# Plain FFN phases of a transformer on one core: up products with the tokens as weights, their result turned later

## The reference, cut to what matters

```python
D_MODEL, SEQ, D_FF = 1024, 256, 2816

def swiglu(h, wg, wu, wd):
    return (jax.nn.silu(h @ wg) * (h @ wu)) @ wd

h = modulate(rms_norm(x, ln_ffn1[i]), sh1, sc1)
x = x + 0.5 * g1[:, None, :] * swiglu(h, ffn1_wg[i], ffn1_wu[i], ffn1_wd[i])
```

## Time and profile before

| what | us |
|---|---|
| median of 3 runs | 1723.72 (1723.26 to 1723.75) |
| the profiled execution, its own time | 1719.21 |
| its span, first to last instruction | 1717.5 |
| TensorE busy in the span | 1690.1 (98%) |
| VectorE busy | 1395.2 (81%) |
| ScalarE busy | 908.7 (53%) |
| mean DMA traffic over the span | 257 GB/s |

### The profile page before, as it was taken

The page is one execution under the profiler, slowest core; times in us unless marked ns, Lnnn a source line. Parts: engine busy times, 40 slices in busy tenths (PEclk is TensorE's granted clock), DMA queues, the critical chain, the costliest instruction groups (busy, mean ns, idle before and its releaser), DMA issues. The chain is left out here.

```text
span 1717.5 us, 35012 instructions
## 1 busy us (share of the span) xinstructions
PE 1690.1 (98%) x13871; PEld 1649.3 (96%) x13871; DVE 1395.2 (81%) x1785; ACT 908.7 (53%) x1274; POOL 327.8 (19%) x517
## 2 busy tenths in 40 slices
PE   7999999999999999999999999989999999999999
PEld 6999999999999999999999999989999998799998
DVE  6777898788779977898987798779988997787655
ACT  3433367764345634366633457657444567774443
POOL 6111110011112111120111125530111132300000
PEclk9999999999999999999999999999999999999999
DMA  9999967649998899977799965235999882358550
GB/s 338 369 378 331 328 206 265 204 157 351 337 338 286 287 328 316 337 251 260 276 337 341 334 229 196 100 123 171 338 339 329 255 215 69 110 173 288 178 171 24
DMA packets 266302, 440.78 MB, mean 257 GB/s; under 512 B 19278, under 2 KB 201758, under 8 KB 266072
## 3 DMA queue, kind: packets, MB, share of 16 engines
q1 hardware_dynamic: 224968, 290.67, 51.1%
q0 software_dynamic: 41200, 148.71, 23.5%
q10 hardware_dynamic: 32, 0.01, 0.0%
HBM read 423.59 MB, written 17.31 MB: 257 GB/s over the span
## 5 line engine op out<-in xcount | busy, mean ns | idle before, releaser
L2949 DVE TENSOR_TENSOR lo<-raw,hi 128x2048 fp32r<-128x2048 f32 (+2 forms) x251 | 565.6, 2255 | 169.4 <-ACT hi L2774 168.5
L2774 ACT CAST hi<-raw 128x2048 fp32r<-128x2048 f32 (+2 forms) x266 | 497.8, 1874 | 373.0 <-PE dacc L2441 181.6
L2439 PE MATMUL up<-operand_hi,hi 128*128 128x256 f32 x1952 | 552.8, 283 | 1.4 <-DVE lo L2949 1.4
L2440 PE MATMUL up<-operand_lo,hi 128*128 128x256 f32 x1952 | 552.3, 283 | 0.0
L2441 PE MATMUL up<-operand_hi,lo 128*128 128x256 f32 x1952 | 552.3, 283 | 0.0
L2439 PEld LDWEIGHTS up<-operand_hi,hi 128*128 128x128 f32 x1952 | 374.4, 192 | 2.2 <-DVE lo L2949 2.0
L2441 PEld LDWEIGHTS up<-operand_hi,lo 128*128 128x128 f32 x1952 | 374.5, 192 | 0.0
L2440 PEld LDWEIGHTS up<-operand_lo,hi 128*128 128x128 f32 x1952 | 374.5, 192 | 0.0
L2439 PE MATMUL dacc<-act_hi,hi 128*128 128x256 f32 x976 | 276.8, 284 | 0.2 <-DVE act_lo L3183 0.2
L2441 PE MATMUL dacc<-act_hi,lo 128*128 128x256 f32 x976 | 275.9, 283 | 0.0
L2440 PE MATMUL dacc<-act_lo,hi 128*128 128x256 f32 x960 | 270.5, 282 | 0.0
(11 more groups left out here) (496 smaller groups left out, 2907.5 us busy)
## 6 DMA issues: line engine op xcount, KB each, us to landing
ada<-in_ada_w_dram POOLq DMA_DIRECT2D x224, 512.0 KB, 6.2
raw<-in_ffn_wg_dram SPq DMA_DIRECT2D x88, 512.0 KB, 6.0
raw<-in_ffn_wu_dram SPq DMA_DIRECT2D x88, 512.0 KB, 5.6
raw<-in_ffn_wd_dram SPq DMA_DIRECT2D x88, 512.0 KB, 5.3
raw<-in_ffn_w_up_dram SPq DMA_DIRECT2D x88, 512.0 KB, 4.7
raw<-in_ffn_w_down_dram SPq DMA_DIRECT2D x46, 512.0 KB, 4.6
raw<-in_hg_w_in_dram SPq DMA_DIRECT2D x32, 512.0 KB, 4.8
fold_scratch<-ada_acc POOLq DMA_DIRECT2D x28, 512.0 KB, 6.9
```

Source lines behind the costliest of these rows:

```text
L2439: pe.matmul(o, stat[0], mov[0], start=start, stop=False, skip_group_check=True)
L2440: pe.matmul(o, stat[0], mov[1], start=False, stop=False, skip_group_check=True)
L2774: last = act.copy(put(slab(hi, s, SPL)), take(slab(raw, s, RAW)))
L2949: last = dve.tensor_tensor(put(slab(lo, s, SPL)), take(slab(raw, s, RAW)), put(slab(hi, s, SPL)).bitcast(F32), ALU.subtract)
```

## The change

In the plain phases every up product on the normed operand (11 blocks in F0, blocks 1 to 10 in F1, F2, F3; `by_rows`) has activations as the stationary operand, 128 tokens at a time, and 512 columns streaming: 256 of the gate and 256 of the up weights. A slab now holds four of the eight row blocks of both matrices, not all eight of one; it is loaded by as many DMAs of the same size. Bank t of `up` takes token tile t, its first half the gate and its second half the up part (F0's block 0 uses two banks of `dacc`). 48 matmuls of 512 columns take the place of 96 of 256.

The silu and the product then have tokens on the partitions. `turn` transposes the product, four times 128 x 128, into bank 0 of misc: after the first slab of the next block's up products, and for the last block after the fifth of eight column steps of the down product before its own. `hidden_hi` and `hidden_lo` read that bank in place of `act32`, and move on ScalarE and VectorE into the next block's iteration, ahead of the split of its third slab. The silu waits for both slabs and stands behind that split. TensorE waits for the product of a block before the first slab of the next one. `gain_sum` moves to bank 1 of misc. The ada tiles stand at the end of an iteration, and the last two blocks of a phase come out of the loop.

```diff
+def by_rows(p, i):
+    return p[0] == "F" and not (p in raw_first and i == 0)
...
+def row_banks(p, i, it=0):
+    t = dacc[:, 0:2 * 512] if p not in raw_first and isinstance(it, int) and i == 0 else up[:, :]
+    return t.rearrange("p (t c) -> p t c", t=NT)
...
-    def up_src(p, i, j):
+    def up_src(p, i, j, rows=None):
+        if by_rows(p, 1 if rows is None else rows):
+            g, u = [w.rearrange("(k p) n -> p k n", p=P) for w in ffn_sources(p)[0:2]]
+            return [(lambda t, a=a: t.rearrange("p (k g n) -> p k g n", k=KB // 2, g=2)[:, :, a, :],
+                     w[:, 4 * j:4 * j + 4, bass.ds(i * 256, 256)]) for a, w in enumerate((g, u))]
...
+    def row_ups(s, j, dst, first_of=None):
+        sl = (slab(hi, s, SPL), slab(lo, s, SPL))
+        stat = lambda part, k, t: op_k((operand_hi, operand_lo)[part], k)[:, t * P:(t + 1) * P]
+        mov = lambda q, k: sl[q][:, (k - 4 * j) * 512:(k - 4 * j + 1) * 512]
+        ks = range(4 * j, 4 * j + 4)
+        if first_of is None:
+            order = itertools.product(ks, range(NT)) if j == 0 else [(k, t) for t in range(NT) for k in ks]
+            for k, t in order:
+                for part, q in ((0, 0), (0, 1), (1, 0)):
+                    last = pe.matmul(dst[:, t, :], stat(part, k, t), mov(q, k), start=(k == 0 and part == 0 and q == 0),
+                                     stop=(k == KB - 1 and part == 1), skip_group_check=True)
+            last.then_inc(slab_used, 1)
+            return
+        n = normed_count(first_of) - KB
+        for k in ks:
+            pe.wait_ge(S["norm_hi"], n + k + 1)
+            for t, q in itertools.product(range(NT), range(2)):
+                pe.matmul(dst[:, t, :], stat(0, k, t), mov(q, k), start=(k == 0 and q == 0), stop=False,
+                          skip_group_check=True)
+        for k in ks:
+            pe.wait_ge(S["norm_lo"], n + k + 1)
+            for t in range(NT):
+                last = pe.matmul(dst[:, t, :], stat(1, k, t), mov(0, k), start=False, stop=(k == KB - 1),
+                                 skip_group_check=True)
+        last.then_inc(slab_used, 1)
...
-            if n == KB // 2 - 1 and between is not None:
+            if n == at and between is not None:
                 between()
...
             for j in range(2):
                 s = b + (3 * i - 1 if i else 0) + j
                 slab_ready(s, it)
+                if by_rows(p, i):
+                    first = isinstance(it, int) and i == (1 if p in raw_first else 0)
+                    if not first and j == 0 and not (isinstance(it, int) and i == 1):
+                        pe.wait_ge(S["prod_done"], u + 2 * it)
+                    row_ups(s, j, row_banks(p, i, it), p if first else None)
+                    if j == 0 and i and by_rows(p, i - 1):
+                        turn(i - 1, it)
+                    continue
...
+        def turn(i, it=0):
+            pe.wait_ge(S["prod_done"], count_up(p, i) + 1 + 2 * it)
+            for kk, t in itertools.product(range(2), range(NT)):
+                last = pe.transpose(bank(misc, 0)[:, kk * SEQ + t * P:kk * SEQ + (t + 1) * P],
+                                    act32[:, t * SEQ + kk * P:t * SEQ + (kk + 1) * P], ident[:, :])
+            last.then_inc(S["turned"], 1)
...
-            down_product(s, act_mov(i), False, stop, between)
+            if turning is not None and by_rows(p, turning):
+                down_product(s, act_mov(i), False, stop, lambda: turn(turning, it), at=KB // 2)
+            else:
+                down_product(s, act_mov(i), False, stop, between)
...
         if left_vector(p) is not None:
+            if p in gained:
+                pe.wait_ge(S["row_kept"], gained.index(p) + 1)
             ada_sum(left_vector(p))
         down(1)
-        with pe.Fori(0, (FI - 3) // 2) as it:
+        apart = 2 if by_rows(p, 1) else 0
+        with pe.Fori(0, (FI - 3 - apart) // 2) as it:
...
+        for i in range(FI - apart, FI):
+            ups(i)
+            if p in five_vectors and i == FI - 1:
+                ada_sum(v + 3)
+            down(i - 1, turning=i if i == FI - 1 else None)
...
+        act.activation(gain_row[:, :], gain_place(name), ACT.Sqrt, scale=1.0 / D,
...
-            act.wait_ge(slab_used, s + 1 + RAW * it)
+            act.wait_ge(slab_used, s + (1 if conv else 2) + RAW * it)
...
-                act.activation(silu_sb, bank(up, 0), ACT.Silu).then_inc(S["silu_done"], 1)
+                act.activation(silu_sb.rearrange("p (t n) -> p t n", t=NT), row_banks(p, i, it)[:, :, 0:SEQ],
+                               ACT.Silu).then_inc(S["silu_done"], 1)
...
         def hidden_hi(i, it=0):
+            o = (i % 2) * 2 * SEQ
+            if by_rows(p, i):
+                act.wait_ge(S["turned"], turn_count(p, i) + 2 * it)
+                act.copy(act_hi[:, o:o + 2 * SEQ], bank(misc, 0)).then_inc(S["acthi_done"], 1)
+                return
             act.wait_ge(S["prod_done"], count_up(p, i) + 1 + 2 * it)
-            o = (i % 2) * 2 * SEQ
             act.copy(act_hi[:, o:o + 2 * SEQ], act32).then_inc(S["acthi_done"], 1)
...
+            if not conv:
+                if by_rows(p, i - 1):
+                    hidden_hi(i - 1, it)
+                split_hi(a + 3, it)
+                silu(a, i, it)
+                split_hi(a + 4, it)
+                return
...
         else:
             split_hi(b + 2)
+            split_hi(b + 3)
             silu(b, 0)
-            split_hi(b + 3)
         conv_silu(0)
-        hidden_hi(0)
+        if not by_rows(p, 0):
+            hidden_hi(0)
...
+        if not conv:
+            hidden_hi(FI - 1)
         split_hi_next(p)
...
+            if by_rows(p, i):
+                dve.tensor_tensor(act32.rearrange("p (t n) -> p t n", t=NT), silu_sb.rearrange("p (t n) -> p t n", t=NT),
+                                  row_banks(p, i, it)[:, :, SEQ:2 * SEQ], ALU.mult).then_inc(S["prod_done"], 1)
+                return
...
-            dve.tensor_tensor(act_lo[:, o:o + 2 * SEQ], act32, act_hi[:, o:o + 2 * SEQ].bitcast(F32),
+            dve.tensor_tensor(act_lo[:, o:o + 2 * SEQ], bank(misc, 0) if by_rows(p, i) else act32,
+                              act_hi[:, o:o + 2 * SEQ].bitcast(F32),
                               ALU.subtract).then_inc(S["actlo_done"], 1)
...
             k = some(count[0], k)
+            if by_rows(p, i - 1):
+                hidden_lo(i - 1, it)
             split_lo(a + 3, it)
             k = some(count[1], k)
             product(a + 1, i, it)
             split_lo(a + 4, it)
-            hidden_lo(i, it)
+            if conv or i == FI - 1:
+                hidden_lo(i, it)
             if summed is not None:
...
+        if not by_rows(p, 0):
+            hidden_lo(0)
+        iteration(1, 0, v, 0, (0, 2, 2) if conv else (0, 0, 4), ahead=p in raw_first)
...
+        iteration(2, 0, v, 4, (2, 1, 1) if conv else (0, 0, 4), summed=left_vector(p))
...
+        apart = 2 if by_rows(p, 1) else 0
+        more = p in five_vectors
+        with dve.Fori(0, (FI - 3 - apart) // 2) as it:
             iteration(3, it, v + 1 if more else None, 0, (0, 0, 4), folding=v if more else None)
...
+            iteration(4, it, v + 1 if more else None, 4, (2, 0, 2) if conv else (0, 0, 4), summed=v if more else None)
...
+        for i in range(FI - apart, FI):
+            k = i - (FI - apart)
+            iteration(i, 0, v + 4, 5 * k, (1, 1, 1) if k else (1, 0, 4), folding=None if k else v + 3, summed=v + 3 if k else None)
+            if p in gained:
+                gain_update(p, KB - 2 + k)
```

More of the change, by code:

```diff
@@ L218, in build @@
             ada_step folds fold_summed ada_summed mod_done x_turned squared raw_hi_done raw_lo_done gate_scaled nbias_done up_scaled presummed presummed_g sums_done sums_g_done
-            sqrt_done rstd_done spread gain_ready c_spread row_kept scaled norm_hi norm_lo
+            sqrt_done turned spread start_dve c_spread row_kept scaled norm_hi norm_lo
             bank_done ada_taken ngate_pe out_scaled operand_ready x_done silu_done prod_done acthi_done
@@ L327, in tap, with gain_place @@
             return cols[:, o:o + 1] if isinstance(it, int) else cols[:, bass.ds(it * 4 + o, 1)]
+        def gain_place(p):
+            return bank(misc, 1 if p in FFNS else 0)[:, SEQ:2 * SEQ]
         squares = view(0, 2048)
@@ L2220, in ffn @@
                     if b + j not in early_slabs:
-                        load(b + j, 0, up_src(p, 0, j))
+                        load(b + j, 0, up_src(p, 0, j, 0))
                 for i in (1, 2):
@@ L2503, in raw_products, with down_product @@
                 last.then_inc(slab_used, 1)
-            def down_product(s, mov, start, stop, between=None, order=tuple(range(KB)), bank_free=None):
+            def row_ups(s, j, dst, first_of=None):
[23 more added lines that the diff above has]
+                last.then_inc(slab_used, 1)
```

(21 more changed lines are left out.)

10 lines of the change are left out of this document (5 added, 5 removed).

## The result

The changed kernel takes 1727.34 us (median of 14 runs, 1724.88 to 1729.94) beside 1723.73 for the kernel before on the same chip (14 runs, 1720.53 to 1725.64): a ratio of 1.0022, 95% interval 1.0015 to 1.0030. It is slower by 0.22%, 3.6 us, where 7.2 us less was forecast; the time lies above the range.

The account below looks back on a forecast made before the run. TensorE's stream was taken to bound the plain phases. -25.8 (up products) + 18.0 (turns) + 0.3 + 0.3 = -7.2 us, from 1723.72 to 1716.5 us; range 1713 to 1722.5, chance 0.72.

Parts of the forecast that it names:

- The unrolled last two blocks run the same instructions: Last two blocks of a phase, taken out of the loop: same instructions as the loop, no cost put on them.
- VectorE sums it some 17 us on: nothing: POOL's fold starts some 2.5 us later, with the later ada tiles; VectorE sums it some 17 us on; no cost.
- The up products: TensorE, 41 blocks: 48 matmuls of 512 columns take 10.88 us, 0.63 us less per block, -25.8 us.
- the turns: TensorE, four transposes for each of 41 changed blocks: 0.44 us each, +18.0 us; bounds 0.43 and 0.67.
- a pace of 230 or more: Sign of being wrong: 512-column matmuls on `up` 230 ns or more apart, where 227 was forecast.
- The 4.2 us ahead of the product: Ahead of the next up products: product ready at 12.9, wanted at 17.08, so 4.2 us of cover and no cost.
- the thin one at the phases' ends: Last block of a phase: low part ready at 5.9 against 6.2, 0.3 us of cover; taken as 0, bound 4 x 1 us.
- (a): F0's first block: TensorE's wait for the second slab's low half grows by 0.3 us.
- (b): First changed blocks of F1 to F3: second slab's low half slightly late, a step of perhaps 0.1 us, three times.
- rival 3: Hand-over of the product more than 4.2 us late, half a microsecond in 37 blocks: +18.5, 1735 us; chance 0.06.
- The 2.7 us of cover ahead of the low part: Ahead of the down product: low part ready at 8.6, wanted at 11.32, so no cost.
- for act_lo in the list of waits: Sign of being wrong: TensorE waits for the low part `act_lo` in the list of waits.

Follow-up runs that it names:

- Experiments 1: Changed kernel with block 9's first tile of the fifth vector moved behind the low part and second split: 1718.66 us, ratio 0.9986.
- experiment 6: Changed kernel with two of four tiles in each loop round's second block moved ahead of its product, so the fold is issued sooner: 1714.79 us, ratio 0.9964.
- experiment 5: Changed kernel with the next vector's first tile ahead of the low part in the three loop rounds of each F phase too: 1783.56 us, ratio 1.0364.
- experiment 3: Kernel with block 9's first tile behind the low part, and the 41 turns left out, so the product is not turned: 1700.67 us.
- experiment 2: Changed kernel with all eight tiles of the fifth vector at the ends of blocks 9 and 10, four and four: 1729.54 us, ratio 1.0045.

## Why the prediction was wrong

**The step that failed** is one sentence and half of another: "The unrolled last two blocks run the same instructions", and of POOL's fold "VectorE sums it some 17 us on: nothing". The instructions are the same; their order in VectorE's queue is not. I followed the fold to its reader (the sum) and not to the writer that has to wait for it, the next vector's first tile, which reuses `ada_acc`. Both halves of the warning were in the text: the diff has the counts (1, 0, 4) and (1, 1, 1) for these blocks, and by the earlier trace rows POOL waits up to 6.8 us for a fold to land. A tile whose turn comes 2.3 us after the last one of the vector before can't start then. Price: 8.6 us of TensorE's waits, and 1.5 of clock in that execution. Experiments 1 and 6 take the waits away at either end of the chain, and experiment 5 makes twelve more of them.

**The up products and the turns** were right in kind and too good in size. The gain is 0.12 us a block and not 0.63 - 0.44 = 0.19: 4.9 us instead of 7.8. By experiment 3, 48 wide products take 10.89 to 10.93 us and not 10.88, some 1.2 us over 41 blocks; and a turn between the slabs costs 0.44 as forecast, plus, by the trace, 0.04 to 0.05 in the steps behind it, some 2 us. The prediction named "a pace of 230 or more" as what would show it wrong: the steady step is 227, only some behind each change are more. Within the microsecond to which these sums are known, the two terms explain the difference between the forecast -7.2 and the -3.6 to -4.3 us of the plain phases once the waits are gone (with the turn first, -5.1 and -5.2).

The steady step again does not agree with the rule of the Trainium skill's page "TensorE: Matmul & The Clock Gate", section "Back-to-back issue gap": N / 2.4 + 2.5 ns, which the section calls the gap of an isolated matmul, gives an estimate of 216 ns for 512 columns, where this stream has 227.

**The covers** held. The 4.2 us ahead of the product were real. In F1's block 8 VectorE's product ends at 502.16, and the next up products start at 506.53, 4.4 us later:

```profile
501.47 0.69 DVE L3269 TENSOR_TENSOR work<-work,up 128x512 f32<-128x512 f32 x1 [1.48 <-ACT work L2950]
```

So was the thin one at the phases' ends, 0.3 us, taken as 0: in F1 the turn in the last down product but one stands at 541.89 with no wait before it, the last low part ends at 543.84, and the last down product, which needs it, starts at 544.48 without a wait. F0's first block waits 1.1 us for its second slab's low half, 0.84 before, the +0.3 of (a). Of (b)'s three steps two show, 0.34 us where 0.23 is the rule, at 374.7 in F1 and 843.2 in F3.

**The rivals.** The outcome is nearest to rival 3, "a late ada tile or fold sits in VectorE's" queue, which I priced at the other hand-over (the product) and over 37 blocks. It was the low part, four times 2.15 us: 8.6 in all where I had put 18.5. The 2.7 us of cover ahead of the low part were right for the loop's blocks; nobody is late there. A wait of TensorE "for act_lo in the list of waits" was among the signs of being wrong.

## What to carry to other kernels

When a loop's last rounds are unrolled, compare the order in each engine's queue with that of the loop, entry by entry, and ask of each moved instruction not only who reads its result but which buffer it overwrites and whose transfer still reads that buffer. An instruction that waits for a DMA is better placed behind what another engine waits for, as long as nothing behind it is waited for in its turn (experiment 2), or its transfer is issued sooner (experiment 6). And an accumulator that is carried off by a DMA is busy until that has landed (here 7.8 us after its issue), not until its last addition. Here a gain of 0.12 us a block (4.9 us) was worth less than one wrong place in a queue (8.6), so the exits and entries of a phase deserve as much of a prediction as the loop.

## What was not expected of the hardware

A wait of TensorE of 2 to 6 us can cost more than itself. After some of these waits the granted clock is at the 1.2 GHz level for 3 to 4 us (0.50 and 0.53 in the tables above), and the 48 matmuls behind the wait take 1.5 to 1.8 us more; after others it stays at 2.4 GHz. The length of the wait alone doesn't decide: F2's 2.18 us was followed by such a stretch in the changed kernel, F1's 2.79 was not. The Trainium skill's page "TensorE: Matmul & The Clock Gate", section "What's actually happening", says that a gate passes a part of the pulses by how busy the engine has been of late; the two levels agree with the 0.50 and 1.00 of the tables.

The same makes these profiles differ by about 1.5 us in a stage that the change doesn't touch. In H, TensorE waits 1.84 us for VectorE in both kernels. In the kernel before the products behind it step 0.12, at a granted clock of 1.00:

```profile
1138.85 0.68 PE L1259 MATMUL up<-work 128*128 128x128 f32 x4 [1.84 <-DVE work L1558]
...
1139.61 0.28 PE L2441 MATMUL misc<-hi,operand_lo 128*128 128x256 f32 x1
1139.73 0.28 PE L2439 MATMUL misc<-hi,operand_hi 128*128 128x256 f32 x1
```

and in the changed one 0.21, at 0.50; the same 28 instructions take 4.93 us and not 3.39, 1.5 of the 1.7 us by which H is longer:

```profile
1143.88 1.20 PE L1276 MATMUL up<-work 128*128 128x128 f32 x4 [1.84 <-DVE work L1575]
...
1145.52 0.41 PE L2460 MATMUL misc<-hi,operand_hi 128*128 128x256 f32 x1
1145.73 0.41 PE L2461 MATMUL misc<-lo,operand_hi 128*128 128x256 f32 x1
```
